# Sample attention of a decoder step: scores on 32-row strips, page values as separate transfers on GpSimd's queue, nine visits

## The reference, cut to what matters

```python
c_past  = cache_kv_latent[page_table].reshape(n_seq, n_pages * PAGE_SIZE, KV_LORA_RANK)
kr_past = cache_k_rope[page_table].reshape(n_seq, n_pages * PAGE_SIZE, QK_ROPE_DIM)
s_past = (jnp.einsum('bqhc,bkc->bhqk', q_lat, c_past) + jnp.einsum('bqhr,bkr->bhqk', q_rope, kr_past))
s_new  = ...                       # the same against the sequence's own new row
p = jax.nn.softmax(jnp.concatenate([s_past, s_new], -1) * ATTN_SCALE, axis=-1)
o = jnp.einsum('bhqk,bkc->bqhc', p[..., :P], c_past) + jnp.einsum('bhqk,bkc->bqhc', p[..., P:], c_new)
```

## Time and profile before

| | us |
|---|---|
| timed, median of 3 (lowest to highest) | 734.67 (734.67 to 734.92) |
| the profiled execution | 734.77 |
| its span | 733.0 |
| PE busy | 726.9 (99%) |
| ACT busy | 410.9 (56%) |
| POOL busy | 535.6 (73%) |
| DVE busy | 306.4 (42%) |
| granted clock of PE, mean | 0.999 of 2.4 GHz |

### The profile page before, as it was taken

One profiled execution on the slowest core, in us unless ns is written; L12 is line 12 of the kernel. 1 busy time (PEld: TensorE's weight loads), 2 busy tenths in 40 slices (PEclk: granted clock), 3 DMA queues, 4 the chain that ended last, 5 costly groups with the idle time before them and its releaser, 6 DMA issues.

```text
span 733.0 us, 16735 instructions
## 1 busy us (share of the span) xinstructions
PE 726.9 (99%) x6275; PEld 710.6 (97%) x6275; DVE 306.4 (42%) x774; ACT 410.9 (56%) x749; POOL 535.6 (73%) x254
## 2 busy tenths in 40 slices
PE   9999999999999999999999999999999999999997
PEld 9999999999999999999999888799999999999997
DVE  5446986233332322232588766753232333321101
ACT  7877555455444444555677566564564444444543
POOL 5895778869878888888868122149878887888892
PEclk9999999999999999999999999999999999999999
DMA  7764455656777755666565898326545555555641
GB/s 261 264 206 142 129 168 177 201 173 213 244 235 231 242 182 173 201 202 202 173 257 193 270 373 324 128 63 212 187 146 200 178 194 175 190 180 184 203 160 60
DMA packets 44586, 144.68 MB, mean 197 GB/s; under 512 B 5634, under 2 KB 6018, under 8 KB 44274
## 3 DMA queue, kind: packets, MB, share of 16 engines
q1 hardware_dynamic: 44210, 143.47, 58.6%
q0 software_dynamic: 176, 0.44, 0.2%
q10 hardware_dynamic: 144, 0.02, 0.0%
HBM read 142.42 MB, written 1.48 MB: 196 GB/s over the span
## 4 chain that ended last, share of the span: by engine, by line
PE 95%; ACT 2%; DVE 1%; DMA 1%; issue 0%; SPq 0%; ACTq 0%; DVEq 0%
PE ps L1404 29%; PE ps L1405 29%; PE ps L1406 29%; PE ps L1812 1%; PE ps L1788 1%; PE ps L1732 1%; DMA h<-xT 1%; PE ps L1541 1%; PE ps L1659 0%; PE ps L1450 0%; PE ps L1792 0%; PE ps L1718 0%; ACT whi L500 0%; DVE ps L886 0%; PE ps L1720 0%
## 5 line engine op out<-in xcount | busy, mean ns | idle before, releaser
L427 POOL TENSOR_TENSOR wlo<-raw,whi 128x1024 fp32r<-128x1024 f32 x221 | 527.0, 2408 | 181.6 <-ACT whi L500 181.5
L1404 PE MATMUL ps<-xhi,whi 128*128 128x264 f32 x1000 | 286.3, 286 | 0.0
L1405 PE MATMUL ps<-xlo,whi 128*128 128x264 f32 x1000 | 283.3, 283 | 0.0
L1406 PE MATMUL ps<-xhi,wlo 128*128 128x264 f32 x1000 | 283.2, 283 | 0.0
L500 ACT ACTIVATE whi<-raw 128x1024 fp32r<-128x1024 f32 x221 | 232.7, 1054 | 50.9 <-PE ps L1406 48.6
L1405 PEld LDWEIGHTS ps<-xlo,whi 128*128 128x128 f32 x1000 | 188.5, 189 | 0.1
L1404 PEld LDWEIGHTS ps<-xhi,whi 128*128 128x128 f32 x1000 | 188.3, 188 | 0.3
L1406 PEld LDWEIGHTS ps<-xhi,wlo 128*128 128x128 f32 x1000 | 187.5, 188 | 0.0
L1404 PE MATMUL ps<-ahi,whi 128*128 128x264 f32 x352 | 100.0, 284 | 0.0
L1406 PE MATMUL ps<-ahi,wlo 128*128 128x264 f32 x352 | 99.9, 284 | 0.0
L1405 PE MATMUL ps<-alo,whi 128*128 128x264 f32 x352 | 99.9, 284 | 0.0
(11 more groups left out here) (281 smaller groups left out, 1156.4 us busy)
## 6 DMA issues: line engine op xcount, KB each, us to landing
raw<-w_stream SPq DMA_DIRECT2D x221, 512.0 KB, 3.3
pg<-pages SPq DMA_DIRECT2D x64, 288.0 KB, 4.4
pg<-w_ukT SPq DMA_DIRECT2D x1, 2048.0 KB, 9.2
pg<-w_uv SPq DMA_DIRECT2D x1, 2048.0 KB, 9.3
h<-xT SPq DMA_DIRECT2D x4, 264.0 KB, 4.5
raw<-w_stream SPq DMA_DIRECT2D x4, 256.0 KB, 5.0
wsraw<-wsT SPq DMA_DIRECT2D x1, 512.0 KB, 5.2
bsb<-bs SPq DMA_DIRECT2D x1, 512.0 KB, 5.5
```

The costliest lines, as they stand in the source:

```text
L427: pool.tensor_tensor(wlo[:, c % RING, :], raw[:, c % RING, :], whi[:, c % RING, :].bitcast(F32), ALU.subtract).then_inc(lo_ready, 1)
L1404: pe.matmul(out, whi_, mhi, start=start, stop=False)
L1405: pe.matmul(out, whi_, mlo, start=False, stop=False)
L1406: return pe.matmul(out, wlo_, mhi, start=False, stop=stop)
```

## The change

- **Scores.** Each strip holds 32 rows instead of 16 and 128 columns instead of 256: rows 0 to 15 are the heads against the first 64 positions of a page, rows 16 to 31 against the other 64. The latent queries are stored as 48 columns with the queries in the middle 16 and zeros around them; a window of 32 columns puts them on the first or the second 16 rows, and both halves add into the same PSUM rows, four products of 128 columns on each strip. The rotary queries are block-diagonal, the two halves of the page's positions on the two halves of the partitions: one product of 128 columns instead of two. The clears ahead of both arrays are of the whole arrays.
- **Maximum.** VectorE reduces 128 columns, moves the result by 16 partitions inside each 32 (`stream_shuffle`) and takes the minimum of the two (of negated maxima). The exponential and its sum are over 128 columns; the join of the sums adds two terms a strip.
- **Turned probabilities.** One transpose and one copy of 128 columns.
- **Values.** The latent for `sample_attend` comes from its own array, `page_values`, 64 rows of 512 values a page, so that the 128 partitions of a product are 64 positions of each of a strip's two pages. SyncE issues them for sequences 0 and 1, behind the page's keys; GpSimd issues them for the others, each behind a table lookup of its own, between splits: `values_of(2)` behind the third slab of the output product, `values_of(s)` behind attend `s - 3` (its `spv_done`), with one split behind each of sequences 2 and 4 to 7.
- **Visits.** `sample_slot(s)` is attend `s - 1` and then scores `s`. END of pair 5 holds the last attend; the three visits with an attend alone at the end of pairs 1, 2 and 4 are gone, and these attends stand at the head of the next middle visit. `sample_out(s - 1)` moves on ScalarE to just ahead of the exponential of `s`.
- `total_hi` and `total_lo` move into a gap of the memory plan; some semaphores of the join are merged.

```diff
-        END = (1, None, None, 5, None, None, None, None)
+        END = (1, None, None, 5, None, NS, None, None)
@@ GpSimd
-            splits(PR_S, SLABS)
+            def values_of(s):
+                for g in range(PAGES):
+                    at = s * PAGES + g
+                    load_values(pool, s, g, pool.value_load(tab[0:1, at:at + 1], min_val=0, max_val=PHYS - 1), values_ready)
+
+            splits(PR_S, PR_S + AHEAD)
+            pool.wait_ge(ql_done, 2)
+            values_of(2)
+            splits(PR_S + AHEAD, PR_S + AHEAD + 1)
+            for s in range(3, NS):
+                pool.wait_ge(spv_done, s - 2)
+                values_of(s)
+                if s in (4, 5, 6, 7):
+                    splits(PR_S + AHEAD + s - 3, PR_S + AHEAD + s - 2)
+            splits(PR_S + AHEAD + NS - 3, SLABS)
@@ VectorE
-                    dve.memset(qsr[ROPE:P, 0], 0.0).then_inc(qsr_done, 1)
-                    dve.memset(qsr[0:ROPE, 1], 0.0).then_inc(qsr_done, 1)
+                    dve.memset(qsr[:], 0.0).then_inc(qsr_done, 1)
+                    dve.memset(qsl[:], 0.0).then_inc(qsr_done, 1)
...
-                dve.tensor_reduce(nms[:, s:s + 1], ps[:, 5, 0:2 * P], AX, ALU.max, negate=True).then_inc(snm_done, 1)
+                dve.tensor_reduce(nmx[:, 0:1], ps[:, 5, 0:P], AX, ALU.max, negate=True).then_inc(snx_done, 1)
+                dve.wait_ge(snx_done, 2 * s + 1)
+                dve.stream_shuffle(nmx[:, 1:2], nmx[:, 0:1], TURN16).then_inc(snx_done, 1)
+                dve.wait_ge(snx_done, 2 * s + 2)
+                dve.tensor_tensor(nms[:, s:s + 1], nmx[:, 0:1], nmx[:, 1:2], ALU.min).then_inc(snm_done, 1)
@@ PE, sample_scores
-                    for j in range(4):
-                        pe.matmul(strip(j), qsl[:, c, s, :], pg[:, b, 2 * j:2 * j + 2, c * P:(c + 1) * P], start=c == 0,
-                                  stop=False)
-                for z in range(2):
-                    for j in range(4):
-                        last = pe.matmul(strip(j)[:, :, z * ROPE:(z + 1) * ROPE], qsr[:, z, s, :],
-                                         pg[:, b, 2 * j:2 * j + 2, LAT:KEYT], start=False, stop=z == 1)
+                    for z in range(2):
+                        queries = qsl[:, c, s, H - z * H:3 * H - z * H]
+                        at = c * P + z * HALF
+                        for j in range(4):
+                            pe.matmul(strip(j), queries, page_keys[:, b, 2 * j:2 * j + 2, at:at + HALF],
+                                      start=c == 0 and z == 0, stop=False)
+                for j in range(4):
+                    last = pe.matmul(strip(j), qsr[:, s].rearrange("p z h -> p (z h)"),
+                                     page_keys[:, b, 2 * j:2 * j + 2, LAT:KEYT], start=False, stop=True)
@@ PE, the loop over pairs
                 values(p)
-                if p and END[p - 1] is not None:
-                    sample_attend(END[p - 1])
                 if MID[p] is not None:
-                    sample_scores(MID[p])
+                    sample_slot(MID[p])
...
                 attend(p)
-                if MID[p] is not None:
-                    sample_attend(MID[p])
                 if END[p] is not None:
-                    sample_scores(END[p])
+                    sample_slot(END[p])
```

More of the change, by code:

```diff
@@ L252, in build @@
         pages_ready = [sem(f"pages_ready{r}") for r in range(BUFS)]
+        values_ready = [sem(f"values_ready{r}") for r in range(BUFS)]
         v_saved, ckr_saved, y_saved, ys_saved = map(sem, ("v_saved", "ckr_saved", "y_saved", "ys_saved"))
@@ L828, in _ @@
                 exponentials(p, 0)
-                if p and END[p - 1] is not None:
+                if p and END[p - 1] in range(NS):
                     sample_turned(END[p - 1])
@@ L839, in _ @@
                 values_high(p)
-                if p and END[p - 1] is not None:
-                    sample_out(END[p - 1])
                 if p == JOIN + 1:
@@ L1385, in _ @@
                 heads_low(p)
-                if END[p] is not None:
+                if END[p] in range(NS):
                     sample_maximum(END[p])
@@ L1800, in turn_probs, with sample_slot @@
                     pe.wait_ge(ptc_done, s)
-                for b in range(2):
-                    last = pe.transpose(ps[:, 6, 2 * b * P:(2 * b + 1) * P], ps_[:, b * P:(b + 1) * P], ident[:])
-                last.then_inc(spt_done, 1)
+                pe.transpose(ps[:, 6, 0:P], ps_, ident[:]).then_inc(spt_done, 1)
             def sample_attend(s):
                 pe.wait_ge(ptc_done, s + 1)
+                if s > 1:
+                    pe.wait_ge(values_ready[s % BUFS], 16 * PAGES * (s // BUFS + (s % BUFS == 2)))
                 if s:
                     pe.wait_ge(os_done, s)
-                for b in range(2):
+                for z in range(2):
                     for j in range(4):
-                        last = pe.matmul(ps[32 * j:32 * j + H, 7, 0:LAT], pT[:, b, 32 * j:32 * j + H],
-                                         pg[:, s % BUFS, 2 * j + b, KEYT:PAGE], start=b == 0, stop=b == 1)
+                        at = (2 * j + z) * H
+                        last = pe.matmul(ps[32 * j:32 * j + H, 7, 0:LAT], pT[:, at:at + H], page_vals[:, s % BUFS, j, z, :],
+                                         start=z == 0, stop=z == 1)
                 last.then_inc(spv_done, 1)
+            def sample_slot(s):
+                if s:
+                    sample_attend(s - 1)
+                if s < NS:
+                    sample_scores(s)
             def totals():
```

106 lines of the change are left out of this document (61 added, 45 removed).

## The result

The changed kernel takes 745.51 us (median of 4 runs, 744.14 to 746.46) against 734.67: 1.0143 times as long, 95% interval 1.0131 to 1.0155. The forecast was 732.4. The profiled execution took 745.18, with a span of 743.6, 10.6 more than before.

What follows compares the result with a forecast made beforehand. PE's issue was taken to bound the attention stage. Scores 1.47, transposes 0.77 and visits 0.29, less 0.20 for sequence 0, gave 2.3 us: 734.7 - 2.3 = 732.4, with an 8-in-10 range of 731.0 to 738.0.

Steps and rivals of the forecast that it cites:

- the forecast said 0.46: Behind pairs 1, 2 and 4, without lone attends: about 0.46 us from last attend product to second product of next scores.
- the sum said 0.20: Sequence 0, in pair 0: the longer maximum chain is not hidden, so it loses 0.20 us; bounds -0.3 to +0.4.
- the sum said 2.3: Total gain: scores 1.47, transposes 0.77, visits 0.29, less 0.20 for sequence 0, together 2.3 us.
- their term: Three lone attend visits removed: 0.81 us saved, 0.52 given back waiting for the keys' low half, 0.29 left.
- the edits costed at nothing: Larger clears, extra SyncE value issues, same page bytes, sequence 6 keys landing by 447 for use at 450: no cost.
- The sign of a wrong forecast: A PE gap in front of an attend, at middle visit 5 or behind it, would make the forecast wrong.
- The rival that came near: GpSimd's value queue is late, splits and lookups in series: 737.6 us at 1.10 a transfer, 746 at 1.32; chance 0.22.
- the 461 that the prediction asked for: GpSimd's value issues about 1.1 us apart, the last of them before 461.
- 3.4: Rival: all of the gain stays, no wait at the three places or in pair 0; 731.4 us, chance 0.10.
- 1.0: Rival: waits eat the gain, chains pass PE by 0.2 at each middle visit; 733.8 us, chance 0.13.
- 0.216: Rival: a score set on 32 rows takes a 256-column set's 0.216 us whatever its columns; 740.8 us, chance 0.02.
- 777: Rival: GpSimd's 40 value transfers paid one after another take 92 us, 44 too many; time near 777, chance 0.03.

Runs made afterwards that it cites:

- e10_splits_moved: e7_gather_tail with three of GpSimd's splits in the attention stage moved elsewhere between the gathers: 732.82 us.
- e7_gather_tail: Changed kernel with values of sequences 2 to 7 fetched by four gathers each, last output issued by ScalarE, first sample maximum in PSUM: 732.74 us.
- e4_wide_values: Changed kernel with GpSimd's value transfers of sequences 3 to 7 going to all 128 partitions, 1024 B each, instead of 64 with 2048 B: 738.30 us.
- e2_tiny_values: Changed kernel with GpSimd's value transfers of sequences 3 to 7 moving 4 rows of a page instead of 64, same number and places: 736.49 us.
- e5_tail: Changed kernel with the last output issued and awaited by ScalarE instead of GpSimd: 743.22 us.

## Why the prediction was wrong

**What held.** The pace of PE and, within some tenths, the terms taken from it. The products of 128 columns on 32 rows: 0.87 for the 32 instructions, 0.109 a set (439.54 to 440.41). The rows behind pair 1, where the earlier trace rows had 1.42 and the forecast said 0.46:

```profile
425.66 0.27 PE L1441 MATMUL ps<-xhi,xlo 128*128 128x128 f32 x1
425.92 0.39 PE L1753 MATMUL ps<-xhi,ohi 128*128 128x256 f32 x1
426.14 0.22 PE L1754 MATMUL ps<-xhi,olo 128*128 128x128 f32 x1
```

are 0.48 apart, with the wait for the low half of the keys, whose VectorE step ends at 425.87. Behind the first scores, sequence 0's transpose starts 0.15 later than in the earlier trace rows, and its attend 0.17 later than before, where the sum said 0.20:

```profile
411.42 0.28 DVE L1337 TENSOR_REDUCE nmx<-ps 128x1 f32<-128x128 f32 x1
411.75 0.15 DVE L1339 STREAM_SHUFFLE nmx<-nmx 128x1 f32<-128x1 f32 x1
411.93 0.16 DVE L1341 TENSOR_TENSOR nms<-nmx 128x1 f32<-128x1 f32 x1
...
412.64 0.33 PE L1838 MATMUL ps<-ident,sq 128*128 128x128 f32 x1 [0.18 <-ACT sq L836]
```

With the loss taken away the stage is 72.93 to 73.01 instead of 74.94: 2.0 gained where the sum said 2.3. The step that a split holds off accounts for the difference: 0.41 in pair 2, by e10_splits_moved. e7_gather_tail takes 732.74, near the 732.4 of the forecast, and that is in part luck: the held-off step costs it 0.4, the visits gave 0.1 more than their term, and its end is 0.2 shorter by the moved output, which the forecast did not have.

**The step that failed** stands among the edits costed at nothing: "The bytes of a page are the same", and the keys of sequence 6 land "4.4 later, so 447 at the latest". The release was right (438.5 forecast; 439.9 in a run that began 1.34 late). The landing was not: 13.7 instead of 4.4. I took the median landing of the earlier trace rows, over all stages, as a constant; the eighth pages of sequences 3 to 7 already took 5.5 to 7.8 in this stage before. The DMA engines' share was 0.95 from 415 to 455 in the kernel before (the row under e4_wide_values) and 1.02 from 424 to 444, so whatever takes them longer there waits in line:

```profile
424.00:434.00 10.00, 10.00 (x113) 8.56 (x113) 6.91 (x25) 6.92 (x20) 2.38 (x1) 1.00 1.02 374
434.00:444.00 10.00, 10.00 (x113) 8.57 (x113) 7.13 (x25) 6.95 (x20) 2.39 (x1) 1.00 1.02 379
```

I had read that table for PE alone. With the same bytes in more packets (14.4 us of engine time a page instead of 13.3) the keys were still in time; to 64 partitions, beside which keys and slabs take longer, they were not. The sign of a wrong forecast that the prediction named, a gap of PE in front of an attend, came as 0.36 only; the gap of 5.8 stood in front of scores.

**What was left out** altogether: the closing drain, 2.0 at the end, since 48 transfers more on GpSimd's queue were priced at their issue alone, and the low clock behind a wait, 2.2, which makes a wait of 6 us cost 8.

**The rival that came near** had the price of GpSimd right: 1.10 forecast, 1.15 measured between two issues (rows below). But no run shows GpSimd late: in e2_tiny_values, with as many issues as far apart, the last leaves at 460.44, ahead of the 461 that the prediction asked for, and attend 7 does not wait. The waits for values (0.36 here, 1.83 in e4_wide_values) came from landings of 7.7 and 8.0, where the prediction took 3.3 to 4.3. The time that this rival would give, 737.6 to 746, holds the result, but by another mechanism: the keys were late, by their landing.

```profile
417.90 0.52 POOL L339 DMA_DIRECT2D pg<-page_values  x1 [0.26 <-issue]
419.04 0.52 POOL L339 DMA_DIRECT2D pg<-page_values  x1 [0.62 <-issue]
```

The sum of it, from the forecast's span on: 733.0 - 2.0 gained + 1.3 at the start (not the change) + 6.8 waits + 2.2 low clock + 2.0 drain = 743.3, of the 743.6 measured.

The remaining rivals fell: the gain was 2.0, neither 3.4 nor 1.0; sets of scores take 0.109, not 0.216, and transfers on GpSimd's queue overlap, so nothing is near 777.

## What to carry to other kernels

Before a transfer is moved or split, read the share of the DMA engines and the landing times in the stretch where it runs, not over the whole kernel: at the 0.95 of this stage the landing time was that of a queue, and transfers to half of the partitions took more of the engines than their bytes say (247 ns a packet instead of 199) and delayed those beside them. A queue on GpSimd had two prices here, the lookup and issue, and a drain at the program's end; and where its splits fall decides which steps of VectorE they hold off. A wait of PE of several microseconds is to be priced with the low clock behind it.

## What the runs showed that I had not expected

- The closing drain of GpSimd grows by 82 ns for each transfer it issued (0.39 for 4, 2.36 for 28, 4.32 for 52), whatever their size (4.32 with 4 rows instead of 64). Where ScalarE issues the last output, it is 0.3 longer for one transfer less (4.61 in e5_tail, 2.65 in e7_gather_tail); why, no run shows.
- A VectorE step of one or two columns can take 0.4 to 2.5 us while a split of GpSimd runs, and ends with it: the minimum with both inputs in SBUF (2.46 in e2_tiny_values, 1.41 in e4_wide_values) and the scaling (1.14 in e7_gather_tail). The shuffle, with one input in SBUF, took 0.15 inside a split (e4_wide_values, 462.83). The Trainium skill, page "SBUF — State Buffer", section "SBUF: two separate sides", names a pair of ports that the two engines lock against each other, for VectorE steps with two SBUF inputs and for those in a mode that uses two ports. The traces agree for the minimum: with one operand in PSUM it took 0.16 inside a split (e10_splits_moved, 451.59). In which mode the scaling runs, no run shows.
- A gather of 128 rows of 2048 B takes GpSimd 0.95 and stands 1.25 from the next, for twice the bytes of a lookup and a plain transfer at 1.15.
